# Reordering evictions, gate work, transposes and one seam in a two-layer GLA / HGRN2 decoder step

## The reference

```python
h = h + 0.5 * swiglu(rms_norm(h, ffn1_norm), w_gu, w_down)     # d_ff 2816
h = h + mixer(rms_norm(h, mix_norm))       # layer 0: GLA, 4 heads; layer 1: HGRN2, 8 heads
h = h + 0.5 * swiglu(rms_norm(h, ffn2_norm), w_gu, w_down)
gate = sigmoid(rms_norm(h, ple_norm) @ ple_w_gate)
h = h + gate * (p @ ple_w_proj)            # gated per-layer input embedding
```

```python
b = cumsum(gc)                                       # log gates
attn = einsum(q, k, exp(b_t - b_s)) masked           # inside a chunk
o = attn @ v + (q * exp(b)) @ S
S = S * exp(b_last) + (k * exp(b_last - b)).T @ v
```

## Time and profile before

| | |
|---|---|
| median of 3 runs | 2303.7 us (2302.86 to 2304.66) |
| profiled execution, own time | 2301.7 us |
| its span, first to last instruction | 2299.8 us |
| TensorE busy | 2245.3 us (98%), 17519 products |
| VectorE busy | 1585.8 us (69%) |
| ScalarE busy | 1086.9 us (47%) |
| GpSimd busy | 441.0 us (19%) |
| mean granted TensorE clock | 0.994 of full |
| an FFN weight unit, issue to landing | 5.1 us |

### The profile page before, as it was taken

How to read it: one execution, slowest core, us unless ns; L and a number is a source line. 1 busy time by engine, 2 the same in 40 slices (tenths; PEclk the granted TensorE clock), 3 DMA queues, 4 the chain that set the end, 5 groups by cost and what they waited for, 6 DMA issues and landing times. The chain is left out here.

```text
span 2299.8 us, 41766 instructions
## 1 busy us (share of the span) xinstructions
PE 2245.3 (98%) x17519; PEld 2190.4 (95%) x17519; DVE 1585.8 (69%) x2132; ACT 1086.9 (47%) x1567; POOL 441.0 (19%) x283
## 2 busy tenths in 40 slices
PE   7999999999999999999999999998998999999998
PEld 6999999989899999999999999997988899999998
DVE  7888833557568888535788883459578678886344
ACT  5555622343545555323555562264365455555234
POOL 5222201112021221201122220104022112222001
PEclk9999999999999999999999999999999999999999
DMA  3434332224242333333233333322232323333331
GB/s 114 111 93 110 95 101 81 84 74 121 68 126 82 96 107 99 97 90 93 63 104 105 98 97 99 82 82 65 81 104 78 91 80 99 103 95 99 102 93 49
DMA packets 385752, 213.33 MB, mean 93 GB/s; under 512 B 6959, under 2 KB 379342, under 8 KB 385566
## 3 DMA queue, kind: packets, MB, share of 16 engines
q1 hardware_dynamic: 385344, 210.59, 32.3%
q0 software_dynamic: 32, 0.03, 0.0%
q10 hardware_dynamic: 190, 0.05, 0.0%
HBM read 198.98 MB, written 11.67 MB: 92 GB/s over the span
## 5 line engine op out<-in xcount | busy, mean ns | idle before, releaser
L598 PE MATMUL ps<-u_diffs,w_high 128*128 128x272 f32 x2560 | 487.4, 288 | 2.7 <-ACT ps L1161 2.7
L598 PEld LDWEIGHTS ps<-u_diffs,w_high 128*128 128x128 f32 x2560 | 401.5, 188 | 3.5 <-issue 3.5
L2176 POOL TENSOR_TENSOR hidden<-t_gate,t_up 128x544 f32<-128x544 f32 x88 | 228.7, 2599 | 764.2 <-ACT t_gate L1184 764.2
L598 PE MATMUL ps<-u_diffs,w_low 128*128 128x272 f32 x1280 | 368.9, 288 | 0.0
L1546 DVE TENSOR_TENSOR w_low<-w_raw,w_high 128x1024 fp32r<-128x1024 f32 x205 | 263.8, 1304 | 97.0 <-ACT w_high L1062 96.8
L545 PE MATMUL ps<-hid_high,w_high 128*128 128x272 f32 x1408 | 291.2, 288 | 3.8 <-DVE w_low L1546 2.1
L545 PE MATMUL ps<-hid_high,w_low 128*128 128x272 f32 x1408 | 289.5, 288 | 0.0
L545 PE MATMUL ps<-hid_low,w_high 128*128 128x272 f32 x1408 | 289.2, 287 | 0.0
L598 PE MATMUL ps<-u_high,w_low 128*128 128x272 f32 x960 | 278.2, 290 | 0.0
L598 PE MATMUL ps<-u_low,w_high 128*128 128x272 f32 x960 | 276.0, 287 | 0.0
L598 PE MATMUL ps<-u_high,w_high 128*128 128x272 f32 x960 | 274.9, 286 | 0.7 <-DVE w_low L1642 0.7
(11 more groups left out here) (262 smaller groups left out, 4218.0 us busy)
## 6 DMA issues: line engine op xcount, KB each, us to landing
w_raw<-in_ffn_w_gu_dram SPq DMA_DIRECT2D x176, 512.0 KB, 5.1
w_raw<-in_ffn_w_down_dram SPq DMA_DIRECT2D x64, 512.0 KB, 4.6
w_raw<-in_hgrn_w_in_dram SPq DMA_DIRECT2D x32, 512.0 KB, 4.2
w_raw<-in_gla_w_in_dram SPq DMA_DIRECT2D x25, 512.0 KB, 4.2
w_raw<-in_ffn_w_down_dram SPq DMA_DIRECT2D x32, 384.0 KB, 4.2
w_raw<-in_ple_w_gate_dram SPq DMA_DIRECT2D x16, 512.0 KB, 4.6
states_s<-in_state_gla_dram SPq DMA_DIRECT2D x8, 512.0 KB, 5.6
out_gla_s_dram<-states_s SPq DMA_DIRECT2D x8, 512.0 KB, 3.5
```

The costliest lines, as they stand in the source:

```text
L598: mm = pe.matmul(ps[:, bank, 0:HALF], half_slot(w, base, h)[:, k * P:(k + 1) * P], x(k), start=start and k == 0 and part == 0, stop=k == K ...
L2176: pool.tensor_tensor(HID[:, f, :], tG[:, :], tU[:, :], ALU.mult).then_inc(s["hid_mul"], 1)
```

## The change

Six edits, all of order and waits, and one of engine; the arithmetic is the same.

1. `ffn`: the last hidden tile's product is made by VectorE after `hid_low(11)`, not by GpSimd.
2. GLA group 0: the diagonal waits for three gate biases (`x_out` 3), the fourth is waited for before value tile 4; VectorE evicts gate bias 3 and the diagonal before `level_diffs`, in all groups.
3. HGRN groups: `gate_end` stands ahead of the weight conversion at feature 7.
4. HGRN groups: g2's eviction comes straight after the last `level_gates`, ahead of two weight conversions and the suffix sums; the two conversions follow the sums.
5. NH = 4: the second eight transposes stand between value tiles 1 and 2.
6. Layer 0's `ple`: the last unit counts `u_free` after each of its eight k tiles, and ScalarE and VectorE make `u_high` and `u_low` of the next FFN as they come free; the weight conversion there goes to the end.

```diff
@@ TensorE
-        def products(..., cut=HALF):
+        def products(..., cut=HALF, read=None):
...
+                if read is not None and k < nk - 1:
+                    mm.then_inc(read, 1)
...
                 if u == 0 and c == 4:
                     pe.wait_ge(s["diag_out"], gr.gi + 1)
+                    if gr.has_r:
+                        pe.wait_ge(s["x_out"], 4)
...
             if gr.has_r:
-                pe.wait_ge(s["x_out"], 4)
+                pe.wait_ge(s["x_out"], 3)
...
             for j in range(4):
+                if NH == 4 and j == 2:
+                    pe.wait_ge(s["kd_out"], N_KD[gi] + 1)
+                    keys(1)
...
-            if NH == 4:
-                pe.wait_ge(s["kd_out"], N_KD[gi] + 1)
-                keys(1)
@@ ScalarE, ple
+            def next_high(tiles):
+                for k in tiles:
+                    act.wait_ge(s["u_free"], k + 1)
+                    high_out(e + 1, k)
+
             for i, m in enumerate(PLE_ORDER):
-                ahead(n + i)
+                last = l == 0 and m == KT_D - 1
+                if not last:
+                    ahead(n + i)
...
+                if last:
+                    next_high(range(4))
                 if m >= 2:
                     square_out(e + 1, m - 1)
...
-                if m == KT_D - 1 and l == 0:
-                    act.wait_ge(s["mm_units"], n + len(PLE_ORDER))
-                    high_out(e + 1, 0)
+                if last:
+                    next_high((4, 5))
                 act.wait_ge(s["ple_t"], 8 * l + m + 1)
                 act.activation(GT[:, m, :], GT[:, m, :], ACT.Sigmoid).then_inc(s["ple_sig"], 1)
             if l == 0:
-                for m in range(1, 4):
-                    high_out(e + 1, m)
+                next_high((KT_D - 2,))
+                act.wait_ge(s["mm_units"], n + len(PLE_ORDER))
+                act.wait_ge(s["h_done"], 8 * (e + 1) + KT_D)
+                high_out(e + 1, KT_D - 1)
             square_out(e + 1, KT_D - 1)
             if l == 0:
-                for m in range(4, KT_D):
-                    high_out(e + 1, m)
+                ahead(n + len(PLE_ORDER) - 1)
@@ VectorE, ffn
+            def last_hidden():
+                dve.wait_ge(s["prod_out"], nth(F, 4, NK - 1, 4))
+                dve.wait_ge(s["silu_done"], NF * (F + 1))
+                dve.wait_ge(s["hid_mul"], NF * (F + 1) - 1)
+                dve.tensor_tensor(HID[:, NF - 1, :], tG[:, :], tU[:, :], ALU.mult).then_inc(s["hid_mul"], 1)
...
             for f in range(10, NF):
                 hid_low(f)
+                if f == 11:
+                    last_hidden()
@@ VectorE, features
+                if not gr.gla and j == 7:
+                    gate_end(gr)
                 ahead(n)
                 if gr.gi == 1 and j == 1:
                     log_sigmoid(gr)
-                if not gr.gla and j == 7:
-                    gate_end(gr)
...
-                        level_diffs(gr, 1)
                         if gr.has_r:
                             gates_out(gr, (3,))
                         diagonal(gr)
+                        level_diffs(gr, 1)
...
             level_gates(gr, 6)
-            ahead(n + 1)
+            if gr.gla:
+                ahead(n + 1)
+            else:
+                feature_out(gr, gr.nfeat + 2, gr.g3_unit - 1, OG[:, 4 * gr.g + 2, :])
@@ VectorE, mix
-            ahead(gr.g3_unit)
+            if gr.gla:
+                ahead(gr.g3_unit)
...
-            feature_out(gr, gr.nfeat + 2, gr.g3_unit - 1, OG[:, 4 * gr.g + 2, :])
+            if gr.gla:
+                feature_out(gr, gr.nfeat + 2, gr.g3_unit - 1, OG[:, 4 * gr.g + 2, :])
+            else:
+                ahead(gr.g3_unit - 1)
+                ahead(gr.g3_unit)
@@ VectorE, ple
+                if last:
+                    tile_low(e + 1, 0)
                 if m >= 2:
                     residual(m - 1)
+                if last:
+                    for k in range(1, 4):
+                        tile_low(e + 1, k)
...
-            tile_low(e + 1, 0)
+            if l == 0:
+                tile_low(e + 1, 4)
+                tile_low(e + 1, 5)
             residual(KT_D - 1)
-            for m in range(1, KT_D):
+            for m in range(KT_D - 2, KT_D):
                 tile_low(e + 1, m)
+            if l == 0:
+                ahead(n + len(PLE_ORDER) - 1)
@@ GpSimd, ffn
-            for f in range(NF):
+            for f in range(NF - 1):
```

More of the change, by code:

```diff
@@ L264, in _build @@
         "sq_mm sq_out ks_made seqmask_made os_out o_out osq_made var_mm var_ln ors_made og_pre og_silu og_made og_made_p out_hi out_lo ple_t ple_sig "
-        "p_turned p_feat p_hi p_lo p_out ple_mm ple_x y_even y_made y_turned ssq_turned y_out_a y_out_v"
+        "p_turned p_feat p_hi p_lo p_out ple_mm ple_x u_free y_even y_made y_turned ssq_turned y_out_a y_out_v"
     ).split()
@@ L535, in unit_ready, with products @@
             pe.wait_ge(s["lo_made"], n + 1)
-        def products(slot, nk, k0, kt_total, bank, xh, xl, m0=0, kw=P, before=None, w0=0, cut=HALF):
+        def products(slot, nk, k0, kt_total, bank, xh, xl, m0=0, kw=P, before=None, w0=0, cut=HALF, read=None):
             for k in range(nk):
@@ L964, in ple @@
                         pe.wait_ge(s["ple_t"], 8 * l + m - 3)
-                    products((n + i) % RING, KT_D, 0, KT_D, 2 * (m % 4), UH, UL, before=wait_u(e) if m == 0 else None)\
-                        .then_inc(s["mm_units"], 1)
+                    products((n + i) % RING, KT_D, 0, KT_D, 2 * (m % 4), UH, UL, before=wait_u(e) if m == 0 else None,
+                             read=s["u_free"] if l == 0 and m == KT_D - 1 else None).then_inc(s["mm_units"], 1)
                 if m == 0:
@@ L1486, in ple @@
             if l == 0:
-                for m in range(1, 4):
-                    high_out(e + 1, m)
+                next_high((KT_D - 2,))
+                act.wait_ge(s["mm_units"], n + len(PLE_ORDER))
+                act.wait_ge(s["h_done"], 8 * (e + 1) + KT_D)
+                high_out(e + 1, KT_D - 1)
             square_out(e + 1, KT_D - 1)
             if l == 0:
-                for m in range(4, KT_D):
-                    high_out(e + 1, m)
-            else:
+                ahead(n + len(PLE_ORDER) - 1)
+            if l == 1:
                 scaled_out(KT_D - 1)
@@ L1953, in gate_end @@
             k = gr.gi - 1
+            dve.wait_ge(s["kx_made"], k)
             dve.wait_ge(s["gd_ln"], k)
```

## The result

The changed kernel takes 2272.67 us (median of 4 runs, 2271.24 to 2274.66), the kernel before 2303.28 us on the same chip (4 runs, 2300.11 to 2304.66): a ratio of 0.9868, 95% interval 0.9855 to 0.9880, so 30.6 us less where 23.0 were forecast. The forecast of 2280.7 us had the direction right. The lower end of its range, 2276.5 us, was 3.8 us too high, and even its 3% for more gain than forecast reached down only to 2274. The profiled execution took 2271.89 us (2301.7 before), its span is 2270.2 us (2299.8 before).

The account below looks back on a forecast made before the run. TensorE, busy 98% of the span, was taken as the bound, with VectorE's chain setting the HGRN level stretch. Savings of 3.8 + 1.6 + 15.0 + 2.6 = 23.0 us off 2303.7 gave 2280.7 us, range 2276.5 to 2288.

Parts of the forecast that it names:

- Step 4: Diagonal's eviction before level_diffs, two HGRN groups: removes a 0.65 us wait, net 0, bounds -0.5 and +0.65 us per group.
- rival D: HGRN level chain blocked by GpSimd, so slower: up to 20 us more per group, 2308.7 us at 14; chance 3%.
- Step 1: Last up product on VectorE, four FFNs: 0.95 us each, 3.8 us in all, bounds 0 and 3.8.
- Step 2: Diagonal of GLA group 0: the wait for head 3's gate bias moves to value tile 4, gain 1.6 us.
- Step 3: gate_end put ahead in two HGRN groups: 1.3 us gained at the diagonal and kept by the VectorE chain behind it.
- Step 5: Third gate eviction ahead of chunk sums, two HGRN groups: the 4.26 us wait goes, a new 1.0 us wait comes.
- Step 6: Key transposes split, HGRN groups: the 1.1 us wait for their copy is hidden behind two products.
- Step 7: Embedding seam: next FFN's second unit 3.0 us sooner, about 0.4 us given back; gain 2.6 us, bounds 0 and 3.2.
- Rival A: TensorE's clock doesn't recover after the remaining stalls: two or three dips take 4 to 5 us, 2285 us; chance 12%.
- B: HGRN VectorE chain takes the front edits' gain back, growing by 1 us per group: 2285.3 us; chance 9%.
- C: Seam does nothing, or one four-fold 0.95 us stays: 2.6 to 3.8 us less gain, 2283.3 to 2284.5 us; 7%.
- E: A moved wait holds TensorE exactly where the old one did: within noise, 2303.7 us; chance 2%.

Follow-up runs that it names:

- e3: The kernel before with only the diagonal's eviction put ahead of level_diffs in the HGRN groups: 2299.25 us, ratio 0.9981.
- e4: The changed kernel with level_diffs put back ahead of the diagonal's eviction in the HGRN groups: 2275.23 us, ratio 0.9878 to the kernel before.

## Why the prediction was right and where it failed

**Step 4 failed**, and it is the largest part of the miss: 4.0 us of the 7.6 between 23.0 and 30.6. It said "the VectorE chain has the same work in another order [...] Net 0, bounds -0.5 and +0.65 per group". The same work in another order is 2.0 us per group shorter (e3, e4), three times the upper bound. The forecast took a VectorE instruction's length as its own. It knew better further on: rival D counted 6.2 us per group lost on `level_gates` to GpSimd, and wrote against itself that "the order within each level is unchanged". It is not unchanged: step 4 puts a PSUM eviction where GpSimd works on `q_tilde` and two-input instructions where it doesn't. D had the right mechanism with one sign only. Asking which VectorE row stands beside GpSimd, before and after, would have shown it: beside the 64-wide difference of 1.21 us at 1549.91 stands another 64-wide instruction with two SBUF inputs that takes 0.21 us, at 1560.42, when GpSimd is done. The 0.4 us that the HGRN sum took off because the chain "will not meet GpSimd at the same points" had the wrong sign for the same reason.

**Step 1 failed in size.** The stalls' idle time was taken for their cost: 0.95 forecast, 1.47 measured, 2.2 us over four FFNs. The extra 0.26 us per stall was in the rows of before. The product's 0.7 us (0.72 measured), the free place in VectorE's queue and the third down unit's slack held:

```profile
271.74 0.72 DVE L1688 TENSOR_TENSOR hidden<-t_gate,t_up 128x544 f32<-128x544 f32 x1
```

**The same omission, smaller, in steps 2, 3 and 5**: 1.75 for 1.6, twice 1.47 for 1.3, twice 4.55 (without the order's part) for 4.26: 1.1 us over them.

**Steps 3, 5 and 6 were right** in mechanism. Step 3's gain is kept by the chain. Step 5's wait goes whole, the walk's order and lengths hold, and the new wait is there, 0.6 and not 1.0 us long. Step 6 gives 1.28 for a wait of 1.1. The three come to 16.5 us where 15.0 was taken and 15.4 computed.

**Step 7 was right**: 2.35 for 2.6. Waits of 1.02 us (0.8 + 0.1 forecast) for `u_low` and 0.19 (0.5 forecast) for the sum of squares:

```profile
1115.00 0.52 PE L545 MATMUL ps<-u_high,w_high 128*128 128x272 f32 x2 [1.02 <-DVE u_low L1573]
...
1117.18 1.18 PE L562 MATMUL ps<-ssq,ones 128*128 128x272 f32 x4 [0.19 <-POOL ssq L2206]
```

**The clock.** Rival A is out as it was priced: both gate units run at the full level. But "another dip gone", which the range allowed for, and a new one both happened: -1.65 at the output projection, +0.93 at 1616, +0.67 at the start, and +0.86 from 2257.9 us on, where TensorE's last 29 products start within 6.43 us instead of 5.57. Together they are 0.8 us against the change in this profile. Where they fall is luck, not a part of the change.

**The account**: 23.0 forecast + 4.0 (order, step 4) + 2.2 (step 1) + 0.15 (step 2) + 1.5 (rest of HGRN) - 0.25 (seam) = 30.6; less 0.8 for the clock, 29.8, against 29.6 us of span. Rivals B, C and E are out, and D as it was stated. That TensorE's waits "fell by less than 12 us" didn't happen (21.2), and L1888's and L1904's successors didn't grow by 0.3 us.

**Left open**: what decides whether the clock falls behind small products. At 621.7, 1616.2 and 1760.6 us it fell at the same place of its group's work, and two executions of one and the same kernel don't show it in the same groups.

## What to carry to other kernels

Where VectorE's chain sets the end, as in these level stretches, its rows beside GpSimd have to be read as "length plus what GpSimd holds": look for instructions that take a microsecond more than their twins, and put evictions from PSUM, not two-input SBUF work, where GpSimd is busy. A TensorE stall cost more than its idle row here, by 0.15 to 0.3 us each; compare the distance from the last product before it to the second after it with an undisturbed one. And when a wait is shortened, list what else hung on the same semaphore: here 0.8 us made the state loads the next wait, and issuing half of them earlier took it away.

## What of the hardware was not expected

- A GpSimd product of 128x544 takes 1.67 us where VectorE pauses (0.43 of it still beside VectorE's last subtraction) and 8.51 beside its back-to-back two-input subtractions, which lose nothing themselves (0.65 us from start to start in both). The loss isn't shared.
- A VectorE instruction of 64 columns (0.21 us) takes 1.21 to 1.31 beside a two-input GpSimd product, and 0.21 just behind a GpSimd memset at the same place.
- TensorE's first pair of 272-column products takes 0.49 to 0.52 us instead of 0.41 behind a stall of half a microsecond as behind one of 1.02; it takes 0.50 at 1592.89 us too, behind products of another shape and with no idle time.
